# Input projection of a hybrid layer as one step of Strassen's product, in two passes of 1024 tokens

## The reference

```python
h = x @ w_in                                   # 2048 x 1024 by 1024 x 2760
q, k, v, z, b, a, c_q, c_kv, k_r = jnp.split(h, IN_SPLITS, axis=-1)
qkv = jax.nn.silu(causal_dwconv(jnp.concatenate([q, k, v], -1), conv_w))   # 4 taps, per channel
... gated delta rule on q, k, v (gated by silu(z)) | multi-head latent attention on c_q, c_kv, k_r
mix = jnp.concatenate([o_gdn, o_mla], -1) @ w_out
x = layer_norm(ALPHA * x + mix)
x = layer_norm(ALPHA * x + (silu(gate) * up) @ w_down)      # gate, up = split(x @ w_gate_up)
out = x + sigmoid(x @ w_ple_gate) * (p @ w_ple)
```

## Time and profile before

| | us |
|---|---|
| median of 3 runs | 3541.81 |
| lowest, highest | 3540.32, 3545.20 |
| profiled execution | 3540.79 |
| its span (first to last instruction) | 3539.3 |
| TensorE busy | 3218.3 (91%) |
| DVE, ACT, POOL busy | 1689.5, 1131.5, 1037.2 |
| mean granted TensorE clock | 0.961 of full |

### The profile page before, as it was taken

How to read it: one execution, slowest core, us unless ns; L and a number is a source line. 1 busy time by engine, 2 the same in 40 slices (tenths; PEclk the granted TensorE clock), 3 DMA queues, 4 the chain that set the end, 5 groups by cost and what they waited for, 6 DMA issues and landing times. The chain is left out here.

```text
span 3539.3 us, 48206 instructions
## 1 busy us (share of the span) xinstructions
PE 3218.3 (91%) x16244; PEld 2679.7 (76%) x16244; DVE 1689.5 (48%) x2776; ACT 1131.5 (32%) x2514; POOL 1037.2 (29%) x863
## 2 busy tenths in 40 slices
PE   7999987779999689796997999989999799999798
PEld 5888864568888577685875888878888588888576
DVE  3652004346666555554567554585555433333433
ACT  2111014334444355454224333343333311111321
POOL 2222212033333176652006333363333100000222
PEclk9999998989999899998998999999999899999899
DMA  3212124311111311102553322212222533333433
GB/s 137 77 71 83 71 97 129 118 54 48 45 52 28 84 57 43 53 21 94 176 168 137 123 78 89 79 64 89 78 82 65 190 101 97 97 93 98 161 120 105
DMA packets 263069, 323.20 MB, mean 91 GB/s; under 512 B 15152, under 2 KB 205616, under 8 KB 258480
## 3 DMA queue, kind: packets, MB, share of 16 engines
q1 hardware_dynamic: 211544, 239.09, 21.2%
q0 software_dynamic: 18144, 66.07, 5.2%
q10 hardware_dynamic: 33280, 16.78, 1.7%
...
...
## 5 line engine op out<-in xcount | busy, mean ns | idle before, releaser
L1942 PE MATMUL ff_bank<-ff_x_hi,ff_w_lo 128*128 128x512 f32 x1240 | 489.1, 394 | 34.3 <-DVE ff_w_lo L2122 19.7
L1943 PE MATMUL ff_bank<-ff_x_lo,ff_w_hi 128*128 128x512 f32 x1240 | 488.0, 394 | 0.0
L1944 PE MATMUL ff_bank<-ff_x_hi,ff_w_hi 128*128 128x512 f32 x1240 | 487.6, 393 | 0.0
L1925 POOL TENSOR_TENSOR ff_w_sum<-ff_w_raw 128x512 f32<-128x512 f32 x210 | 294.3, 1411 | 504.3 <-DVE ff_w_lo L2122 443.3
L1942 PEld LDWEIGHTS ff_bank<-ff_x_hi,ff_w_lo 128*128 128x128 f32 x1240 | 236.0, 190 | 86.7 <-DVE ff_w_lo L2122 22.8
L2322 PE MATMUL fd_acc<-fd_w_hi,fd_a_lo 128*128 128x512 f32 x704 | 278.0, 395 | 25.4 <-DVE fd_a_lo L2306 25.4
L176 PE MATMUL in_h_ps<-in_x_hi,in_w_lo 128*128 128x512 f32 x704 | 276.8, 393 | 25.5 <-POOL in_w_lo L153 25.5
L177 PE MATMUL in_h_ps<-in_x_lo,in_w_hi 128*128 128x512 f32 x704 | 276.2, 392 | 0.0
L178 PE MATMUL in_h_ps<-in_x_hi,in_w_hi 128*128 128x512 f32 x704 | 276.2, 392 | 0.0
L2324 PE MATMUL fd_acc<-fd_w_hi,fd_a_hi 128*128 128x512 f32 x704 | 275.8, 392 | 0.0
L2323 PE MATMUL fd_acc<-fd_w_lo,fd_a_hi 128*128 128x512 f32 x704 | 275.8, 392 | 0.0
...
## 6 DMA issues: line engine op xcount, KB each, us to landing
ff_w_raw<-w_gate_up SPq DMA_DIRECT2D x44, 1024.0 KB, 5.2
scratch_hT<-in_out SPq DMA_DIRECT2D x22, 1024.0 KB, 3.8
fd_a_raw<-scratch_hid SPq DMA_DIRECT2D x176, 128.0 KB, 2.1
...
scratch_hid<-ff_first SPq DMA_DIRECT2D x44, 256.0 KB, 2.3
scratch_hid<-ff_second SPq DMA_DIRECT2D x44, 256.0 KB, 2.3
in_x_raw<-xT SPq DMA_DIRECT2D x8, 1024.0 KB, 4.8
```

Of the source, the lines that this page charges most:

```text
L1925: pool.tensor_tensor(w_sum[:, SUM_SLOT[m]], w_raw[:, b, one], w_raw[:, b, two], op).then_inc(w_sum_done, 1)
L1942: pe.matmul(acc, w_lo[:, wm, ws], x_hi[:, xm, k], start=first_mm, stop=False, skip_group_check=skip)
L1943: pe.matmul(acc, w_hi[:, wm, ws], x_lo[:, xm, k], start=False, stop=False, skip_group_check=skip)
L1944: return pe.matmul(acc, w_hi[:, wm, ws], x_hi[:, xm, k], start=False, stop=last_mm, skip_group_check=skip)
```

## The change

`project_in` is written anew, after the manner of `feed_in`. A pass (p) has 1024 tokens, a unit (u, or f within its pass) one pair of feature tiles: unit 0 plain (copied tiles), 1 silu, 2 and 3 convolution, 4 silu, 5 to 8 convolution, 9 and 10 copied. All loops are written out. Weights are split by ACT and DVE, their sums are made by POOL, all loads and stores are issued by SP. The ring of token sums has 2 slots (`feed_in` has 3).

The convolution is made per pair and pass. A CONV unit's results go into `h_pad` (2 rows of 3 + 1024 tokens), by DVE's adds and ACT's two evictions. Tap 0 is made by ACT (`tap`, 128x1024), the three others by DVE (`conv_taps`): those of row 0 at the unit's end, those of row 1 in the next unit, where also the silu over both rows (`conv_end`, 128x2048) and one store of 1 MB follow. The last three tokens of a pass are kept in `halo`. There is one `conv` tile, and it and `h_pad` lie on `x_raw`, so that the tokens of the second pass are loaded in unit 9 after the last convolution is stored. Other units store `first` and `second`, 256 KB each, two times.

```diff
+    PROD = 7
+    SUMS = 5
+    RING = 2
+    PLAIN, CONV, SILU, COPY = range(4)
+    PAIRS = ((T_CQ // 2, PLAIN), (T_Z // 2, SILU), (0, CONV), (1, CONV), (T_Z // 2 + 1, SILU), (2, CONV), (3, CONV),
+             (4, CONV), (5, CONV), (T_CQ // 2 + 1, COPY), (T_CQ // 2 + 2, COPY))
+    NP = len(PAIRS)
+    UNITS = [(p, f, pair, kind) for p in range(NPASS) for f, (pair, kind) in enumerate(PAIRS)]
...
-        x_raw = s.sb("x_raw", [P, 2, SEQ])
-        x_hi = s.sb("x_hi", [P, KD, SEQ], F32R)
-        x_lo = s.sb("x_lo", [P, KD, SEQ], F32R)
...
+        w_sum = s.sb("w_sum", [P, 3, HW])
+        dif = s.sb("dif", [P, NTOK])
+        first = s.sb("first", [P, NTOK])
+        second = s.sb("second", [P, NTOK])
         taps = s.sb("taps", [P, T_Z * CONV_WIDTH])
-        h_pad = s.sb("h_pad", [P, SEQ + CONV_WIDTH - 1])
-        zero = s.sb("zero", [P, 1])
...
+        flat = x_raw[:].rearrange("p q k t -> p (q k t)")
+        h_pad = flat[:, NTOK:NTOK + 2 * (PAD + TOK)].rearrange("p (m t) -> p m t", m=2)
+        conv = flat[:, 4 * KH * NTOK - 2 * TOK:].rearrange("p (m t) -> p m t", m=2)
+        bank = s.ps("bank", [P, 2, 4, NTOK])
...
+        W_SUM = {0: (A21, A22, ALU.add), 2: (A11, A22, ALU.add), 3: (A12, A22, ALU.subtract),
+                 5: (A11, A12, ALU.add), 6: (A21, A11, ALU.subtract)}
+        X_SUM = {1: (B12, B22, ALU.subtract), 2: (B11, B22, ALU.add), 3: (B21, B22, ALU.add),
+                 4: (B21, B11, ALU.subtract), 6: (B11, B12, ALU.add)}
...
+        PREP_BEFORE = (("w", 0), ("w", 1), ("x", 1), ("w", 2), ("x", 2))
+        PREP_AFTER = (("w", 3), ("w", 4), ("x", 4), ("w", 5), ("w", 6))
...
+            def load_x(p):
+                for n, kh, half in ((B11, 0, 0), (B21, 1, 0), (B22, 1, 1), (B12, 0, 1)):
+                    if p:
+                        sp.wait_ge(conv_stored, 16 * convs(NP * p))
+                        sp.wait_ge(halo_step, 2 * convs(NP * p))
+                        sp.wait_ge(x_lo_done, XP * p)
+                    src = xT[:, KH * kh:KH * kh + KH, TOK * p + NTOK * half:TOK * p + NTOK * (half + 1)]
+                    sp.dma_start(x_raw[:, n], src).then_inc(x_loaded[n], 16)
...
+            def store_conv(u):
+                p, f, pair, kind = UNITS[u]
+                sp.wait_ge(conv_silu, convs(u) + 1)
+                dst = hT[2 * pair:2 * pair + 2, :, TOK * p:TOK * (p + 1)].rearrange("m p t -> p m t")
+                sp.dma_start(dst, conv).then_inc(conv_stored, 16)
...
+            load_w(1)
+            for u, (p, f, pair, kind) in enumerate(UNITS):
+                if u + 2 < NU:
+                    sp.wait_ge(w_lo_done, PROD * (u + 1))
+                    load_w(u + 2)
+                if u and UNITS[u - 1][3] == CONV:
+                    store_conv(u - 1)
+                if f == 9 and p + 1 < NPASS:
+                    load_x(p + 1)
+                if kind == PLAIN:
+                    sp.wait_ge(evicted, evictions(u) + 1)
+                    store(u, 0, 0, first, first_stored)
...
+            def x_sums(p, m):
+                one, two, op = X_SUM[m]
+                pool.wait_ge(x_loaded[one], 16 * p + 16)
+                pool.wait_ge(x_loaded[two], 16 * p + 16)
+                for k in range(KH):
+                    n = x_sum_count(p, m, k)
+                    if n >= RING:
+                        earlier, r = divmod(n - RING, SUMS * KH)
+                        pool.wait_ge(x_lo_done, XP * earlier + NRAW + r + 1)
+                    pool.tensor_tensor(x_sum[:, n % RING], x_raw[:, one, k], x_raw[:, two, k], op).then_inc(x_sum_done, 1)
...
+            def w_sums(u, m):
+                if m not in W_SUM:
+                    return
+                if m == 0:
+                    pool.wait_ge(w_loaded[u % 2], 16 * (u // 2 + 1))
+                one, two, op = W_SUM[m]
+                reached(pool, w_lo_done, PROD * u + SUM_FREE[m])
+                pool.tensor_tensor(w_sum[:, SUM_SLOT[m]], w_raw[:, u % 2, one], w_raw[:, u % 2, two], op).then_inc(w_sum_done, 1)
...
+            for p in range(NPASS):
+                for kind, m in PREP_BEFORE + (("x", 3),) + PREP_AFTER + (("x", 6),):
+                    if kind == "w":
+                        w_sums(NP * p + 1, m)
+                    else:
+                        x_sums(p, m)
+                for f in range(2, NP):
+                    for m in range(PROD):
+                        w_sums(NP * p + f, m)
...
+            def bank_free(u):
+                if u >= 2:
+                    reached(pe, post, posts(u - 1))
+                    pe.wait_ge(evicted, evictions(u - 1))
...
+            def unit(u, p, f):
+                bank_free(u)
+                for m, q in enumerate((Q_C21, Q_C12, Q_C22, Q_M3, Q_C21, Q_C12, Q_C22)):
+                    pe.wait_ge(w_lo_done, PROD * u + m + 1)
+                    if m == 4:
+                        pe.wait_ge(m0_kept, strassens(u) + 1)
+                    if m == 5:
+                        pe.wait_ge(post, posts(u) + 1)
+                    if m == 6:
+                        pe.wait_ge(post, posts(u) + 2)
+                    for k in range(KH):
+                        if f == 1 and m in X_SUM:
+                            pe.wait_ge(x_lo_done, x_sum_index(p, m, k) + 1)
+                        last = triple(bank[:, u % 2, q], m, k, m, k == 0 and m < 4, k == KH - 1, m > 3)
+                    last.then_inc(product, 1)
+            for u, (p, f, pair, kind) in enumerate(UNITS):
...
+            def w_high(u, m):
+                if u >= NU or UNITS[u][3] == PLAIN:
+                    return
+                if IS_SUM[m]:
+                    act.wait_ge(w_sum_done, SUMS * strassens(u) + SUM_BEFORE[m] + 1)
...
+                    act.wait_ge(product, PROD * u)
+                else:
+                    act.wait_ge(product, PROD * (u - 1) + m + 1)
+                act.activation(w_hi[:, m], src, ACT.Copy).then_inc(w_hi_done, 1)
...
+            def keep_m0(u):
+                act.wait_ge(product, PROD * u + 1)
+                reached(act, post, posts(u))
+                act.activation(dif[:], bank[:, u % 2, Q_C21], ACT.Copy).then_inc(m0_kept, 1)
...
+            def tap(u, m):
+                pair, c = UNITS[u][2], convs(u)
+                reached(act, conv_stored, 16 * c)
+                col = CONV_WIDTH * (2 * pair + m)
+                act.activation(conv[:, m], h_pad[:, m, 0:TOK], ACT.Copy, scale=taps[:, col:col + 1]).then_inc(tap_step, 1)
...
+            def conv_begin(u):
+                p, f, pair, kind = UNITS[u]
+                c = convs(u)
+                reached(act, halo_step, 2 * c)
+                reached(act, conv_step, 6 * c)
+                act.activation(h_pad[:, :, 0:PAD], halo[:, pair if p else T_Z // 2], ACT.Copy).then_inc(halo_step, 1)
+                act.wait_ge(halo_step, 2 * c + 1)
+                act.wait_ge(evicted, evictions(u) + 2)
+                tap(u, 0)
+            def conv_odd(u):
+                p, f, pair, kind = UNITS[u]
+                act.wait_ge(post, posts(u) + 6)
+                tap(u, 1)
+                act.activation(halo[:, pair], h_pad[:, :, TOK:TOK + PAD], ACT.Copy).then_inc(halo_step, 1)
+            def conv_end(u):
+                act.wait_ge(conv_step, 6 * convs(u) + 6)
+                act.activation(conv, conv, ACT.Silu).then_inc(conv_silu, 1)
...
+            def unit(u, p, f, kind):
+                after_conv = UNITS[u - 1][3] == CONV
...
+                keep_m0(u)
...
+                w_high(u + 1, 0)
+                if after_conv:
+                    conv_odd(u - 1)
+                for m in (1, 2, 3):
+                    w_high(u + 1, m)
+                if next_plain:
+                    w_high_plain(u + 1, 0)
+                    x_high_raw(p + 1, 1)
+                act.wait_ge(post, posts(u) + 4)
...
+                if kind == CONV:
+                    reached(act, conv_step, 6 * convs(u))
+                    reached(act, halo_step, 2 * convs(u))
+                    act.activation(h_pad[:, 1, PAD:PAD + NTOK], bank[:, u % 2, Q_C21], ACT.Copy).then_inc(evicted, 1)
+                else:
+                    reached(act, second_stored, 16 * n)
+                    act.activation(second[:], bank[:, u % 2, Q_C21], func).then_inc(evicted, 1)
+                w_high(u + 1, 4)
+                if after_conv:
+                    conv_end(u - 1)
+                if next_plain:
+                    w_high_plain(u + 1, 1)
+                    w_high_plain(u + 1, 2)
+                    x_high_raw(p + 1, 2)
+                act.wait_ge(post, posts(u) + 5)
+                if kind == CONV:
...
+                    if kind == SILU:
...
+                        act.activation(first[:], first[:], ACT.Silu).then_inc(first_silu, 1)
+                    act.wait_ge(second_stored, 16 * n + 16)
+                    act.activation(second[:], bank[:, u % 2, Q_C12], func).then_inc(evicted, 1)
+                w_high(u + 1, 5)
+                if kind == CONV:
```

(91 more changed lines are left out.)

343 lines of the change are left out of this document (217 added, 126 removed).

## The result

| | before | after |
|---|---|---|
| median (5 runs each, us) | 3541.81 | 3563.72 |
| lowest, highest | 3537.86, 3545.20 | 3558.73, 3566.72 |
| profiled execution, its span | 3540.79, 3539.3 | 3564.51, 3562.8 |
| next stage's first load | 517.63 | 535.38 |

The ratio after to before is 1.006, with a 95% interval from 1.0045 to 1.0075. The change makes the kernel slower by 21.9 us. I had forecast 46 us slower: the sign and most of the places are right, but the forecast is about double what was measured.

What follows compares the result with a forecast made beforehand. The stage was taken as bound by TensorE's matmuls; -54.4 - 7.1 - 14.8 + 34.6 + 12 + 63.8 + 16 - 2 = +48.1 on 3540.8 gave 3588 us, with a range of 3536 to 3616.

Steps and rivals of the forecast that it cites:

- 240 matmuls: Whole input projection: ten Strassen units of 84 and one plain of 96 per pass leave 240 fewer matmuls, -54.4 us.
- head: Stage start: the first matmul starts at 10.2 instead of 17.3, as in the feed-forward stage, -7.1 us.
- old extra: Old input projection: 14.8 us around its matmul time disappear as GpSimd's weight split goes to ACT and DVE, -14.8.
- sums and ring: Units 0 and 1 of each pass: GpSimd's chain of sums +34.6, waits from two slots +12, both passes.
- convolution: Units 4 and 6 to 9: TensorE waits for DVE's post 2, 31.9 us a pass, +63.8 in all.
- loads of pass 2: Unit 10 of the first pass: small store behind four 1 MB loads, pause 13.3 and clock 2.4, +16 us.
- unit 21 and tail: Stage end: an eviction and store become a shorter add and store, -2 us.
- the ring: Token sums: with two slots each sum waits for DVE's subtraction two before it, 0 to 12 us a pass, +12 taken.
- The lap: Convolved units: chain from one post 2 to the next through the single conv tile, 26.0 us, 4.0 from four GpSimd collisions.
- Rival 3: Convolved units: half the collisions, lap 24, unit 4 on time, 3540 to 3566 us; chance 0.15.
- Between 0 and 0.6 for each: Each of 20 token sums a pass waits up to 0.6 us for DVE's subtraction, 0 to 12 us a pass.
- a charge of 2.4 after pauses over 4 us: TensorE: a pause over 4 us is followed by matmuls at the lower clock, adding 2.4 us.

Runs made afterwards that it cites:

- the new order: Kernel after plus two conv tiles, ACT's w_high 4 and 5 and silu reordered, SyncE storing second before the convolution's 1 MB in units without convolution: 3521.73 us.
- the first experiment: Kernel after with two conv tiles, so tap 0 waits for the store two convolutions ago: 3544.10 us, ratio to before 1.0003.
- the experiment with both edits: Two conv tiles, reordered ACT work and SyncE stores, plus second-pass token loads issued from GpSimd's queue: 3514.12 us, ratio to before 0.9916.
- the fastest kernel: Two conv tiles, reordered ACT and stores, loads from GpSimd's queue, plus RING = 3 and token sums on VectorE: 3502.40 us, ratio to before 0.9874.

## Why the prediction was right and wrong

By the steps of the sum, in us. Measured is from the trace of after, from the first matmul to the next stage's first load.

| step | forecast | measured |
|---|---|---|
| 240 matmuls | -54.4 | -54.4 |
| head | -7.1 | -6.3 |
| old extra | -14.8 | -14.8 |
| sums and ring | +46.6 | +41.0 |
| convolution | +63.8 | +39.1 |
| loads of pass 2 | +16 | +14.8 |
| unit 21 and tail | -2 | -1.8 |
| sum | +48.1 | +17.6 |

The next stage's first load moved by 17.75, so the steps account for the stage. **The step that failed is the size of the convolution term**: +63.8 forecast, +39.1 measured, 24.7 of the 30.5 by which the sum is off. The second is the ring. That the whole time is only 24.3 under the forecast is luck: 5.7 us came in later stages that I had put at nothing (see below).

*Convolution.* Its mechanism stood. TensorE's pauses in units 4, 7, 8 and 9 are before the seventh product and released by `post` 2. ACT's tap waits for the store. Two tiles, sums without reads and short steps each took away what it had to. Three things in its size were wrong.
- The lap was forecast at 26.0 and is 23.7 to 24.3: one collision too many (1.3), steps back to back at 1.28 without the 0.15 that I had put between them (0.6), in the longest lap less a slower store (0.7), and small pieces. Units 7 to 9 lose 16.7 in the first pass for 23.4.
- A shorter lap also meets the unit earlier. In unit 4 `post` 2 came 18.0 us after the start and not 20.4. The pause was 1.6 and not 4.2, and the clock stayed, so the unit lost 1.8 for 6.6. Unit 6 lost nothing for 1.9. An error of 2 us in the lap made 5 in a unit, because the charge for the clock hung on it.
- Unit 5 was put at nothing ("follows a unit without convolution and keeps pace") and lost 1.9, before product 4, released by `keep_m0`. The trace has that copy behind ACT's second eviction, and the eviction behind a small store that SyncE had issued after the 1 MB of the convolution. The prediction had looked at DVE's order only. That the one-column steps freed the unit too fits this, and so does the new order, which frees it; no run has that order of the stores alone.

Rival 3, half the collisions, a lap of 24 and unit 4 on time, 3540 to 3566, is near what happened: the collisions cost 2.3 of 4.0 us, in three meetings of four, and 1.6 us of pause were left in unit 4. I gave it 0.15. What was needed for choosing it was in the code: the wait that frees a slot for a sum is DVE's own subtraction, so whether the next one is already running can be read from the queue order of DVE. I charged a collision for every sum near a subtraction.

*Sums.* 41.0 for 46.6. The forecast from ff without the ring was 34.6, so the ring and all else were 6.4, and a ring of three took back 3.3 at most. "Between 0 and 0.6 for each" double counted: while a sum waits for DVE it does not collide with it, as the 1.91 against 1.70 shows. The rest, 3.1 or more, stays open.

*Loads, head, matmuls, tail.* Within 1.2 us each. The written-out loops cost nothing that can be seen: units 2 and 3 are 19.04.

*Clock.* The rule I used (a charge of 2.4 after pauses over 4 us) had the limit too high and the size only roughly right: after pauses of 3.3 to 3.6 us 7 to 14 matmuls started 0.43 us apart and not 0.23, at the lower clock, and after 2.42 none did. At 0.2 each that is 1.4 to 2.8 us. In short pauses the length alone does not decide. After one of 2.18 in the first experiment's unit 5 six matmuls ran at full speed and eight at the lower clock; after one of 2.76 in unit 11 of the experiment with both edits at most one was slow.

*After the stage.* The span grew by 23.5 and the stage by 17.75. The 5.7 between them arose in stages that the change does not touch. From the next stage's first load to the end of the span there are 3021.7 us in the kernel before, 3027.4 after, and 3020.0 to 3030.3 in the eight experiments, with no order that I can see; the 3030.3 is that of the fastest kernel. So some of the 21.9 may be of this kind. Its cause is open.
